# U and V of a latent pick gathered as one row of 8 KB, and weighed pair by pair behind their dot products

## What is computed

```python
def block(args):
    xb, ib, gb = args
    act = jnp.einsum("td,thkd->thk", xb, u_tab[ib])
    return jnp.einsum("thk,thkd->td", jax.nn.gelu(act) * gb, v_tab[ib])
```

## Time and profile before

| what | value |
|---|---|
| median of 3 runs | 2434.72 us (2434.61 to 2435.57) |
| span of the profiled execution | 2689.8 us |
| DVE busy, share of the span | 57% |
| PE busy | 56% |
| POOL busy | 55% |
| moved by the transfers | 969.43 MB, mean 360 GB/s |
| gathers | 1536, 805.40 MB |

### The profile page before, as it was taken

One profiled execution on the slowest core, in us unless ns is written; L12 is line 12 of the kernel. 1 busy time (PEld: TensorE's weight loads), 2 busy tenths in 40 slices (PEclk: granted clock), 3 DMA queues, 4 the chain that ended last, 5 costly groups with the idle time before them and its releaser, 6 DMA issues.

```text
span 2689.8 us, 20637 instructions
## 1 busy us (share of the span) xinstructions
PE 1510.1 (56%) x6676; PEld 682.0 (25%) x6676; DVE 1524.4 (57%) x4059; ACT 281.3 (10%) x715; POOL 1466.1 (55%) x1540
## 2 busy tenths in 40 slices
PE   6898668694244554554556866868400444442466
PEld 2464433371012110122312442354100100110012
DVE  0349974756886555455360965575776844446401
ACT  1321133010000110100000032211000000000000
POOL 0005445536665666666556635545676666667664
PEclk8889888896666665676768787878755655565568
DMA  9979998988999999999979988888899999999997
GB/s 360 411 320 379 395 388 324 365 306 318 357 397 411 412 388 379 371 410 411 389 286 374 364 341 314 324 313 296 318 399 373 343 383 375 358 374 383 378 357 271
DMA packets 238044, 969.43 MB, mean 360 GB/s; under 512 B 26314, under 2 KB 28746, under 8 KB 227954
## 3 DMA queue, kind: packets, MB, share of 16 engines
q0 software_dynamic: 221184, 805.40, 78.0%
q1 hardware_dynamic: 16754, 162.71, 14.9%
HBM read 964.87 MB, written 3.15 MB: 360 GB/s over the span
## 4 chain that ended last, share of the span: by engine, by line
DVE 27%; PE 24%; issue 15%; POOL 13%; another core or an unknown queue 11%; DMA 7%; ACT 2%; SPq 0%; DVEq 0%; ACTq 0%; POOLq 0%
PE acc L1077 8%; PE psum L1031 6%; DVE ring L1871 6%; POOL work L695 6%; POOL ring L695 5%; DVE work L1871 3%; PE psum L786 3%; DVE work L1463 2%; POOL wring L695 2%; DMA ring<-peer_v_in,vidx 2%; PE psum L796 2%; DVE work L1460 2%; DMA ring<-peer_u_in,idx 1%; DVE wring L1871 1%
## 5 line engine op out<-in xcount | busy, mean ns | idle before, releaser
L695 POOL DMA_INDIRECT ring<-peer_u_in,idx x415 | 396.5, 955 | 460.6 <-DVE idx L1566 208.0
L1871 DVE CUSTOM_DVE_ANT_0 ring<-ring,h_kept 128x1024 f32<-128x1024 f32 x415 | 488.9, 1218 | 126.3 <-DMA ring<-peer_u_in,idx 93.5
L695 POOL DMA_INDIRECT ring<-peer_v_in,vidx x392 | 378.5, 966 | 325.8 <-PE acc L1077 116.9
L1077 PE MATMUL acc<-ring,vw 128*32 128x512 f32 x1412 | 299.2, 778 | 276.6 <-DVE vw L1852 107.6
L1077 PE MATMUL acc<-work,vw 128*32 128x512 f32 x852 | 218.4, 794 | 325.5 <-DVE vw L1852 155.0
L1871 DVE CUSTOM_DVE_ANT_0 work<-work,h_kept 128x1024 f32<-128x1024 f32 x220 | 262.0, 1219 | 159.3 <-DMA work<-peer_u_in,idx 124.2
L695 POOL DMA_INDIRECT work<-peer_v_in,vidx x267 | 252.0, 944 | 144.8 <-issue 74.0
L695 POOL DMA_INDIRECT work<-peer_u_in,idx x220 | 207.1, 941 | 116.7 <-issue 58.9
L1031 PE MATMUL psum<-work,wring 128*128 128x256 f32 (+1 forms) x896 | 187.1, 369 | 49.5 <-issue 46.6
L786 PE MATMUL psum<-wring,work 128*128 128x512 f32 (+1 forms) x432 | 180.4, 575 | 32.4 <-issue 22.8
L1031 PEld LDWEIGHTS psum<-work,wring 128*128 128x128 f32 x896 | 160.3, 216 | 81.5 <-issue 62.0
(11 more groups left out here) (244 smaller groups left out, 2028.4 us busy)
## 6 DMA issues: line engine op xcount, KB each, us to landing
wring<-w_in_in SPq DMA_DIRECT2D x17, 2048.0 KB
wring<-peer_wq_in SPq DMA_DIRECT2D x14, 2048.0 KB
wring<-mod_w_in SPq DMA_DIRECT2D x10, 2048.0 KB
ring<-mod_w_in SPq DMA_DIRECT2D x9, 2048.0 KB, 12.2
wring<-w_out_in SPq DMA_DIRECT2D x8, 2048.0 KB
work<-mod_w_in SPq DMA_DIRECT2D x5, 2048.0 KB, 14.4
ring<-peer_u_in,idx POOLq DMA_INDIRECT x415
ring<-peer_v_in,vidx POOLq DMA_INDIRECT x392
```

Source lines behind the costliest of these rows:

```text
L695: nc.gpsimd.indirect_dma_start(slots[slot_of[n]], None, table, bass.IndirectOffsetOnAxis(ap=at[:, col + r:col + r + 1], axis=0))\
L1077: ins = mm(acc[half][lane:lane + QUAD, :], w[:, at:at + QUAD], two[j - pair][0][:, half * CHUNK:(half + 1) * CHUNK], start=(r == 0), stop= ...
L1871: V.tensor_tensor_reduce(held, held, h_kept[:, :], 1.0, 0.0, ALU.mult, ALU.add, dots[:, dots_at(k, t) + r:dots_at(k, t) + r + 1]).then_inc ...
```

## The change

The two tables are laid out as one, `peer_uv`, in which the V row of an expert stands behind its U row. For the latent steps (1 and 3) one gather now brings both, 8 KB in each partition, 1 MB in all, into two neighbouring slots. The new event kinds are: h, in which PE spreads the normed input of 32 tokens over the partitions into `h_kept` (four times a tile); f, the dot product of one pick; and, behind each two f, e (ACT: gelu of two), m (DVE: gate and spread of two) and p (PE: eight matmuls for two picks). A partition of a row now holds 32 tokens times 4 picks for the dot products too. Context steps gather U and V apart, as before, from the joined table. All matmuls of one group of 32 rows go to the same two lanes. The events of step 1 are spread anew over the pauses of step 2: 198 of its 256 rows up to the last `wq` pause, 26 beside the choosing, 20 behind it, and 12 before the step.

```diff
+DUO = 2
+DUOS = PICKS // DUO
+VW_DUOS = SHARE // DUO
+BESIDE_CHOOSING, BEHIND_CONTEXT = 13, 10
...
+            if stream[n][0] == "f":
+                slot = min((i for i in free if i in wide), key=lambda i: max(last_held(i), last_held(i + 1)))
+                taken_now = (slot, slot + 1)
+            else:
+                slot = min(free, key=last_held)
+                taken_now = (slot,)
...
+                if kind == "f" and r == 0:
+                    pool.wait_ge(*after("both_indexed", k, t))
...
-                table, at = (io["peer_u"], idx) if kind == "u" else (io["peer_v"], vidx)
+                at = idx if kind == "u" else vidx
                 nc.gpsimd.indirect_dma_start(
-                    slots[slot_of[n]], None, table,
+                    row(kind, k, t, r)[0], None, io["peer_both" if kind == "f" else "peer_one"],
...
+            def spread_h(k, t, g):
+
+                pe.wait_ge(u_used, dotted_before["f", k, t, g * QUAD])
+                if g == 0:
+                    pe.wait_ge(*after("h2", k, t))
+                group = slice(g * QUAD, (g + 1) * QUAD)
+                for half in range(2):
+                    o = slice(half * CHUNK, (half + 1) * CHUNK)
+                    ins = mm(h_kept[:, o], c("quads")[group, :],
+                             hn[steps[k].X + t][group, o], start=True, stop=True)
+                ins.then_inc(*mark("h_spread", k, t, g))
...
+                if kind == "p":
+                    if i == 0:
+
+                        pe.wait_ge(*after("acc_free", *previous_tile(steps, k, t)))
+                    pe.wait_ge(*after("vw", k, t, i))
+                    for j in range(DUO):
+                        r = i * DUO + j
+                        g, held = r // QUAD, row("f", k, t, r)[0]
+                        for half in range(2):
+                            lane = QUAD * ((g + 2 * half) % 4)
+                            ins = mm(acc[half][lane:lane + QUAD, :], vw_duo(i)[:, j * QUAD:(j + 1) * QUAD],
+                                     held[:, D + half * CHUNK:D + (half + 1) * CHUNK],
+                                     start=(r % QUAD == 0), stop=(r % QUAD == QUAD - 1))
+                        ins.then_inc(v_used, 1)
...
+                if kind == "e":
+                    at = dots_at(k, t) + i * DUO
+                    act.wait_ge(u_used, dotted_before["f", k, t, (i + 1) * DUO - 1] + 1)
+                    A(dots[:, at:at + DUO], dots[:, at:at + DUO], ACT.Gelu_apprx_tanh).then_inc(*mark("gelu", k, t, i))
...
+            def weigh(k, t, i):
+
+                at, place = dots_at(k, t) + i * DUO, slice(i * DUO, (i + 1) * DUO)
+                dve.wait_ge(*after("gelu", k, t, i))
+                d(V.tensor_tensor(wv[:, place], dots[:, at:at + DUO], gates_of(k, t)[:, place], ALU.mult))
+                settle()
+                if i >= VW_DUOS:
+                    dve.wait_ge(v_used, used_after["f", k, t, (i - VW_DUOS + 1) * DUO - 1])
+                else:
+                    dve.wait_ge(v_used, sums_of(*previous_tile(steps, k, t)) if t == 0 else
+                                used_after["f", k, t - 1, PICKS - (VW_DUOS - 1 - i) * DUO - 1])
+                spread_out = [P, DUO, QUAD]
+                V.tensor_tensor(vw_duo(i).rearrange("p (g t) -> p g t", t=QUAD), quad.unsqueeze(1).broadcast_to(spread_out),
+                                wv[:, place].unsqueeze(2).broadcast_to(spread_out), ALU.mult).then_inc(*mark("vw", k, t, i))
...
+    events = []
     for t in range(st.T):
...
+        for i in range(DUOS):
+            if i * DUO % QUAD == 0:
+                events.append(("h", st.k, t, i * DUO // QUAD))
+            events += [("f", st.k, t, i * DUO + j) for j in range(DUO)]
+            events += [(kind, st.k, t, i) for kind in "emp"]
+        events.append(("x", st.k, t, 0))
+    return events
+
+
+EARLY = 30
...
+    arrays["peer_uv"] = np.stack([inputs["peer_u"], inputs["peer_v"]], 2)
```

More of the change, by code:

```diff
@@ L348, in dots_at, with vw_duo, gates_of @@
             return (sum(st.T for st in steps[:k]) + t) % 2 * PICKS
-        vw_places = [held[:, :] for held in vw] + [region(16384 + i * CHUNK, CHUNK) for i in range(2)]
         def vw_of(k, t, q):
-            return vw_places[q % (4 if k == STEPS - 1 else 2)]
+            return vw[q % 2]
+        def vw_duo(i):
+            at = i % VW_DUOS * DUO * QUAD
+            return vw[0][:, at:at + DUO * QUAD]
+        def gates_of(k, t):
+            at = (steps[k].X + t) * PICKS
+            return idx[:, at:at + PICKS].bitcast(F32)
         def job(pe, *key):
@@ L466, in build_pass @@
         slots = [held[:, :] for held in rows]
+        wide = {n: ring[:, n * D:(n + 2) * D] for n in range(0, RING, 2)}
         extra = []
@@ L471, in spare, with spare_line @@
             slots.extend(views)
[L473 to L480 removed]
+        def spare_line(line, n, first, last):
+            for i in range(0, n - 1, 2):
+                wide[len(slots) + i] = line[:, i * D:(i + 2) * D]
+            spare([line[:, i * D:(i + 1) * D] for i in range(n)], first, last)
+        spare_line(region(10288, 3 * D), 3, after_step[STEPS - 3], after_step[STEPS - 2])
+        spare_line(region(10288 + 3 * D, 4 * D), 4, after_step[STEPS - 3], row_no["u", STEPS - 2, 0, 0])
+        spare_line(region(2 * D, 8 * D), 8, after_step[STEPS - 2], row_no["u", STEPS - 2, 0, 0])
+        for held in wring:
+            spare_line(held, DB * CHUNK // D, row_no["f", STEPS - 1, 0, 0], len(stream))
+        spare_line(region(0, 16 * D), 16, after_step[STEPS - 1], len(stream))
         in_beside, in_left, in_all = RING, RING + 7, RING + 7 + 8 + W_SLOTS * DB * CHUNK // D
@@ L527, in row @@
             n = row_no[key]
-            return slots[slot_of[n]], row_landed[slot_of[n]], 16 * filled[n]
+            return (wide if key[0] == "f" else slots)[slot_of[n]], row_landed[slot_of[n]], 16 * filled[n]
         block = stack.enter_context(nc.Block())
@@ L1477, in regroup, with by_group @@
                         make(to[QUAD * m:QUAD * (m + 1), at + j:at + n:4], j, m)
+            def by_group(make, to, at):
+                for j in range(4):
+                    for m in range(4):
+                        make(to[QUAD * m:QUAD * (m + 1), at + j * QUAD:at + (j + 1) * QUAD], j, m)
             def best_keys(st, t, first, last):
@@ L1861, in gather @@
                 col = n * PICKS
-                if kind == "u":
+                if kind == "h":
+                    if i == 0:
+                        dve.wait_ge(*after("picked", k, t))
+                        settle()
+                        by_group(lambda out, j, m: d(V.tensor_copy(out, gates[QUAD * j:QUAD * (j + 1), col + m:col + PICKS:4])),
+                                 gates_of(k, t), 0)
+                        settle()
+                    dve.wait_ge(*after("h_spread", k, t, i))
+                elif kind == "f":
+                    held, landed, count = row("f", k, t, i)
+                    dve.wait_ge(landed, count)
+                    at = dots_at(k, t) + i
+                    V.tensor_tensor_reduce(held[:, 0:D], held[:, 0:D], h_kept[:, :], 1.0, 0.0, ALU.mult, ALU.add,
+                                           dots[:, at:at + 1]).then_inc(u_used, 1)
+                elif kind == "m":
+                    weigh(k, t, i)
+                elif kind == "u":
                     if i == 0:
@@ L2048, in gather_plans @@
         elif k and k < len(steps):
-            dots = max(n for n, event in enumerate(left) if event[0] == "u") + 1
-            most = dots + int((len(left) - dots) * ROOM)
+            ends = [n + 1 for n, event in enumerate(left) if event[0] == "p"]
+            dots, most = ends[-1 - BESIDE_CHOOSING - BEHIND_CONTEXT], ends[-1 - BEHIND_CONTEXT]
             spread(plan, part(names[0][0], ("wq", 3)), left[:dots])
```

124 lines of the change are left out of this document (54 added, 70 removed).

## The result

| kernel | median (lowest to highest) | runs |
|---|---|---|
| before | 2434.66 us (2432.07 to 2435.57) | 4 |
| changed | 2472.84 us (2470.03 to 2477.71) | 4 |

The ratio is 1.0161, 95% interval 1.0147 to 1.0176. The change costs 1.6%. The forecast was 2410 us and the wrong sign, and 2472.84 lies just above the range.

A forecast was written before the change was run, and what follows sets the result against it. The prediction took DMA transfers, mainly gathers, to bound the kernel. 37 us less in packets and 10 us more in the choosing gave 2663 us profiled, scaled to 2410 us for the median; range 2342 to 2470 us.

The forecast's parts named there:

- The gain in packets: Beside step 2 and in the last stretch: 73728 fewer packets for the same bytes save 13 to 61 us, taken as 37.
- Its a: Fixed time per packet in the DMA queues, beside a time per byte: 13 ns, from the two queues' totals.
- DVE's pair of 3.3 us: DVE's work for two picks: 3.3 us (up to 3.9), covered by 5.3 us of transfers.
- PE's 1.4 us a pair: PE's sums with two lanes working: 0.71 us a row, 1.4 a pair, covered by transfers even at 2.0.
- the first rival: Step 2: DVE, ACT and PE waiting for each other at every pair end last, 1.4 us more each; 2474 us, chance 0.24.
- The 8 wide slots hold 21 us of transfers, more than a dense section lasts: Step 2: the slots' 21 us of transfers were to outlast any dense section, so transfers still end last.
- 68 us to spare: Step 2 up to the last wq pause: 519 us of work against 587 us of transfers, 0.7 us a pair spare.
- The choosing: Step 2's choosing: DVE takes 108 us against 90 us of transfers, a hole of 18 us, 10 counted as new.
- The scaling by 0.905: Whole kernel: sums made against the profiled 2689.8 us, then multiplied by 2434.72 / 2689.8 for the median.
- most holes can't be there: Unprofiled runs: packets alone add up to 2499 us against a 2434.72 us median, so most profiled holes must be absent.
- the third rival: Last stretch and beside step 2: holes close as well, since POOL can catch up after stops; 2339 us, chance 0.16.
- The last doubt of the prediction: Context rows of 4 KB might come slower from a table in which U and V alternate; no size given.

The follow-up runs named there:

- step1_only: The changed kernel with only step 1's rows, gathered beside step 2, joined; step 3's as before the change: 2481.78 us, 1.0207 of the kernel before.
- wide7: The changed kernel with 7 wide slots beside step 2 in place of 8: 2495.71 us on the first kind of chip, 2646.92 us on the second.
- later1: The changed kernel with weights and sums of a pair one pair later, its gelu at once: 2502.72 us, 1.0298 of the kernel before.

## Why the prediction was wrong

**The gain in packets** was right. It said 37 us. The rate went from 409 to 422 GB/s: about 20 us in the last stretch and 14 us in step 2, 34 in all. Its a was 13 ns; by the packet records a 4 KB packet of q0 takes 161 ns and an 8 KB one 312 ns (medians), so two small ones cost 10 ns more than a large one.

**POOL, DVE, PE.** POOL issues a double row in 954 ns on the mean, as assumed. DVE's pair of 3.3 us measured 3.2. PE's 1.4 us a pair was 1.9 us, inside the bound of 2.0. None of these sums is where it went wrong. One row was misread: the earlier trace rows give 1.09 us of idle time before a matmul of 1.01 us, not matmuls 1.09 us apart. In the same trace they begin 2.1 to 2.8 us apart there. It stood only in the first rival. What PE's two lanes do to the holes, no run varied: a pair's sums are 0.5 us longer than the 1.4 assumed, and PE's busy time in step 2 rose by 119 us.

**"The 8 wide slots hold 21 us of transfers, more than a dense section lasts"** is the step that failed. The sum around it (519 us of work against 587 us of transfers, 68 us to spare) compares totals of a whole step, and a total can only be spent if work done ahead is kept somewhere. All that was kept is 8 rows, and these weren't all ahead of the engines: a stop of 14 us was enough for a hole of 5 us (812.7 to 826.7 above), so by this estimate only some 9 us of transfers were still to come when it began, not 21. The other slots held rows that had landed and waited. Before, a row of U was given back by DVE alone and a row of V by PE alone. Now both halves are held from landing until the sums, through DVE, ACT, DVE and PE, each of which may stand in dense work. Between 799 and 1215 us POOL stood over 4.7 us for PE's sums 20 times, up to 17.6 us. `step1_only` places the loss in step 2 (and a little at its ends), `wide7` (27 us for a slot) and `later1` (30 us for a pair held longer) show that it hangs on the slots and how long they are held. More wide slots weren't tried. The averages that I trusted left 0.7 us a pair; what was needed was that no single section be longer than the rows still to come. Of the parts of the circle, the spreads of h (13 us) and the gelu (11) are shown; the wait for PE behind dense matmuls itself is argued from the waits, not isolated.

**The choosing** was mis-sized by a step of its own: "the transfers have 26 rows and 8 slots ahead, 34 x 2.66 = 90 us". The rows that POOL has issued ahead are among the 26, not beside them, since the rows behind the choosing wait for its end. Of the 26, 18 were left to issue when it began. DVE took 88 us, less than the 108 predicted, and still about 35 us of transfers are missing: some 17 in the one wait for the gates, the rest in waits for PE's sums. Predicted was a hole of 18 us, 10 of it new. With 22 pairs 29 us of the program's time came back.

**The end of the program** was left as it was. It got 4.5 us longer.

**The scaling by 0.905**, and with it "most holes can't be there", rested on a wrong idea of why profile and median differed. The last stretch at 374 GB/s was true for its chip. It did the packets' term no harm, but it hid that step 2 ran there at a share of 1.02 with 9 us missing, so that any new hole was a pure loss. On a chip like the one of the trace the change wins, 3.2%, mostly as the third rival said: away from its ends the last stretch goes from 370 to 422 GB/s (2000 to 2300 us in both), and there the holes do close.

**The first rival's 2474 us** was in part luck. It had the right place and the right engines. But its 70 us were an even 1.4 us more at every pair, and moving nine pairs gave 29 us back, which an even cost doesn't. Its base was the trace of the other kind of chip, scaled by 0.905. Its sign, a share of DMA under 0.9 beside step 2, didn't come (0.94), and neither did the forecast's, above 0.95. The last doubt of the prediction, context rows that come slower out of the joined table, has no trace: the dense parts of steps 1 and 3, where they are gathered, take 367 and 401 us before and 367 and 404 after.

**The account** on the first kind of chip: 61 us of missing transfers in step 2, less 34 by the rate, plus 4.5 for the end, is 32; the measured difference of the spans is 40. The windows place the other 8 in the opening (3), in step 3's dense part (3), and in the last stretch.

## What to carry to other kernels

When two buffers with short lives are joined into one with a long life, don't compare total work with total transfers. Compare the longest stretch in which no buffer can be given back with what the buffers hold, and look for it in the releaser's waits; a slot more or less is the quickest test (27 us here). And count what may be issued in a stretch, not what is in flight around it: an in-order queue stops at the first row that isn't allowed yet. Here joining paid where nothing else holds the engines (the last stretch: -0.4%), and cost where dense work stands between landing and release (+2.1%), both on the first kind of chip.

When a trace's span and the median of the runs disagree by 10%, profile again before arguing from either.

## What the runs showed of the hardware

Two kinds of chip, 11% apart for the same kernel (2431 and 2432 against 2688, 2705 and 2700 us). The median 4 KB packet is no slower on the second (159 ns against 161), the mean one hardly (170 against 164). What differs in the last stretch of the kernel before is what PE waits for. One of PE's waits there, on the second kind (1967 to 2600 us):

```profile
PE acc L1077 <- issue: 150.6, 94, 9.2
```

and on the first kind (1760 to 2390 us):

```profile
PE acc L1077 <- DMA ring<-peer_v_in,vidx: 188.5, 34, 107.4
PE acc L1077 <- DMA work<-peer_v_in,vidx: 151.3, 53, 21.1
```

On the first kind PE waits for data. On the second it stands before its next matmul with no releaser that the profile shows, 94 times, and POOL waits longer for its slots, as in the earlier trace rows. With 8 KB rows this wait is nearly gone on the same kind of chip (4.4, 4.1 and 4.5 us for the three groups of sums). What holds PE there while 4 KB rows are gathered, none of these runs shows. It stays open.

The granted clock rose with the change, from 0.55 to 0.75 in the last stretch and from 0.65 to 0.80 in step 2, where PE was busier (238 to 372 and 362 to 480 us); the time didn't follow it. The prediction had expected no other clock.
